# One layer-stack kernel with retrieved experts: a gather carries 32 tokens by four picks instead of 64 tokens by two

## The reference

```
q  = tb @ w_q                        # 8 heads, two halves of 128 each
s1, s2 = q @ keys1, q @ keys2        # 128 keys a half
v1, i1 = top_k(s1, 16); v2, i2 = top_k(s2, 16)
top_s, top_j = top_k(v1 + v2, 16)    # 16 of the 256 pairs, per head
gate = softmax(top_s)
act  = gelu(u_tab[expert] . t) * gate
out  = sum over 8 heads x 16 experts of act * v_tab[expert]
```

## Time and profile before

| what | value |
|---|---|
| median of 3 runs | 3376.12 us (3372.03 to 3384.19) |
| the profiled execution, its own time | 3373.29 us |
| its span | 3371.3 us |
| mean granted TensorE clock | 0.84 of 2.4 GHz |
| PE, DVE, ACT, POOL busy | 2717.7, 2109.5, 1234.6, 1221.1 us |
| moved by DMA | 1225.87 MB, mean 364 GB/s |
| products of `diag` and `ring` | 4096 instructions, 1345.2 us |

### The profile page before, as it was taken

One profiled execution on the slowest core, in us unless ns is written; L12 is line 12 of the kernel. 1 busy time (PEld: TensorE's weight loads), 2 busy tenths in 40 slices (PEclk: granted clock), 3 DMA queues, 4 the chain that ended last, 5 costly groups with the idle time before them and its releaser, 6 DMA issues.

```text
span 3371.3 us, 34626 instructions
## 1 busy us (share of the span) xinstructions
PE 2717.7 (81%) x11134; PEld 1372.6 (41%) x11134; DVE 2109.5 (63%) x4889; ACT 1234.6 (37%) x3752; POOL 1221.1 (36%) x1102
## 2 busy tenths in 40 slices
PE   8789996888988689788977789788788666666777
PEld 7767653444544145344523244344344111111133
DVE  4444688675656786565466785576556776754554
ACT  3211365442333343443333343532333343333332
POOL 0100133553433433334244433343333443433342
PEclk9989997997899689889987799797799676767676
DMA  4205698999999999999999999999999999999998
GB/s 158 75 7 192 232 402 328 392 389 377 411 406 398 391 418 383 383 377 383 413 421 421 393 413 400 376 388 422 378 412 384 390 419 421 376 422 422 421 417 333
DMA packets 186153, 1225.87 MB, mean 364 GB/s; under 512 B 21298, under 2 KB 24130, under 8 KB 50803
## 3 DMA queue, kind: packets, MB, share of 16 engines
q0 software_dynamic: 153024, 1115.00, 81.5%
q1 hardware_dynamic: 32946, 108.66, 8.5%
HBM read 1211.73 MB, written 11.84 MB: 363 GB/s over the span
## 4 chain that ended last, share of the span: by engine, by line
PE 47%; DMA 27%; DVE 15%; ACT 5%; issue 3%; DVEq 2%; POOL 1%; SPq 0%; POOLq 0%; ACTq 0%
PE ps L616 47%; DMA ring<-in_uv,picked 21%; DVE ring L2362 6%; DMA ring<-in_uv,tail_pick 4%; DVEq L2152 1%; ACT scratch L1209 1%; POOL ring L599 1%; ACT gated L1209 1%; ACT diag L1209 1%; DVE scratch L2103 1%; ACT L1209 1%; DMA scratch<-in_keys 1%; ACT act_v L1209 1%; DMA wring<-in_weights 0%; DVE scratch L2107 0%
## 5 line engine op out<-in xcount | busy, mean ns | idle before, releaser
L599 POOL DMA_INDIRECT ring<-in_uv,picked x1024 | 1143.5, 1117 | 1808.3 <-PE ps L616 1712.5
L616 PE MATMUL ps<-ring,diag 128*64 128x512 f32 x4096 | 1345.2, 751 | 490.1 <-ACT diag L1209 486.6
L2362 DVE SCALAR_TENSOR_TENSOR ring<-ring,htok 128x1024 f32<-128x1024 f32 x1024 | 1246.6, 1227 | 702.2 <-DMA ring<-in_uv,picked 697.6
L616 PE MATMUL ps<-hT,wring 128*128 128x256 f32 (+1 forms) x3200 | 797.0, 399 | 18.4 <-DVE hT L1603 8.8
L1209 ACT ACTIVATE act_v<-pre 128x1 f32<-128x1 f32 x1040 | 209.9, 202 | 1555.5 <-DVE ring L2362 1554.5
L616 PEld LDWEIGHTS ps<-ring,diag 128*64 128x64 f32 x4096 | 244.1, 156 | 1197.0 <-ACT diag L1209 1016.0
L616 PEld LDWEIGHTS ps<-hT,wring 128*128 128x128 f32 x3200 | 598.8, 194 | 323.2 <-issue 225.5
L1209 ACT ACTIVATE diag<-folded,gated 128x64 f32<-128x64 f32 x1024 | 356.1, 348 | 33.8 <-PE ps L616 0.4
L1209 ACT ACTIVATE gated<-act_v,gates 128x1 f32<-128x1 f32 x1024 | 301.6, 295 | 33.3
L616 PEld LDWEIGHTS ps<-scratch 128*128 128x128 f32 (+2 forms) x1428 | 207.1, 214 | 152.6 <-issue 89.6
L616 PE MATMUL ps<-scratch 128*128 128x128 f32 (+5 forms) x1428 | 244.2, 317 | 30.0 <-DVE scratch L1750 15.6
(11 more groups left out here) (342 smaller groups left out, 1716.5 us busy)
## 6 DMA issues: line engine op xcount, KB each, us to landing
wring<-in_weights SPq DMA_DIRECT2D x200, 512.0 KB, 7.8
ring<-in_uv,picked POOLq DMA_INDIRECT x1024, 11.8
scratch<-in_keys POOLq DMA_DIRECT2D x4, 1024.0 KB, 10.8
scratch<-in_s_gla POOLq DMA_DIRECT2D x4, 1024.0 KB, 12.3
out_o_gla<-scratch POOLq DMA_DIRECT2D x4, 1024.0 KB, 10.4
scratch<-in_s_dn POOLq DMA_DIRECT2D x1, 2048.0 KB, 12.8
scratch<-in_s_ssm POOLq DMA_DIRECT2D x1, 2048.0 KB, 17.1
out_o_dn<-scratch POOLq DMA_DIRECT2D x1, 2048.0 KB, 11.8
```

The lines of the kernel that those rows point to most:

```text
L599: pool.indirect_dma_start(out=ring[:, g % RING, :], out_offset=None, in_=io["uv"][L], in_offset=bass.IndirectOffsetOnAxis(ap=index, axis=0 ...
L616: return pe.matmul(out, lhsT, rhs, start=start, stop=stop)
L2362: stt(x, x, 1.0, h, MUL, MUL, accum_out=pre[:, g % SMALL:g % SMALL + 1]).then_inc(sem("dotted"), 1)
```

## The change

A gather now carries **32 tokens by four picks** (`FOLD` = 4, `PART` = 32). There are 32 sub-tiles of 32 gathers. `folded` is four identity matrices of 32, `diag` is 128 x 32, and `tile_v` makes four products of 256 columns (`COLS`), into partitions 0 to 31, 32 to 63, 64 to 95 and 96 to 127 of the bank. The token rows must lie four times, so `fold_rows` makes four products per half. A tile's rows are kept as two halves of 64 tokens, a half with its two column parts above each other, in three turning places (`half_rows`, one of them in `otok`). The addition to `xT` moves from slot +4 to +6 and the first fold from +6 to +8. The copies of a choice become 16 for `picked` and 16 for `gates`, of a quarter of the size, over steps 138 to 145. The final norm covers 480 tokens, its second part runs in the last sub-tile, and 32 tokens are left for `last_tile`. `iota` is now a part of `pack`, loaded and not computed. The ring keeps its seven slots.

```diff
-STEPS = 139
+STEPS = 146
+FOLD = 4
+PART = P // FOLD
+NROUND = NPICK // FOLD
+HEAD_ROUNDS = 2 * TOPK // FOLD
+COLS = 1024 // FOLD
+SUBS = FOLD * len(UNITS)
-COPY_AT, TURN_AT, FOLD_AT = 2, 4, 6
+COPY_AT, TURN_AT, ADD_AT, FOLD_AT = 2, 4, 6, 8
...
+        half_rows = (htok[:, 0, 0:512], htok[:, 0, 512:1024], otok[:, 512:1024])
+        diag = sb("diag", [P, DIAGS, PART])
+        folded = sb("folded", [P, PART])
...
-        FINAL = ((0, 256, 12, 784), (256, 192, 15, SUB_FIRST[15] + TURN_AT + 2))
+        FINAL = ((0, 256, 24, 784), (256, 224, 31, SUB_FIRST[31] + ADD_AT + 2))
...
+            def rows_of(bank, at):
+                for c in range(KD):
+                    last = mm(ps[HALF * (c // 4):HALF * (c // 4) + HALF, bank, (c % 4) * P:(c % 4 + 1) * P],
+                              hT[:, c, at:at + HALF], ident)
+                return last
+
             def first_rows():
                 pe.wait_ge(sem("score_ready"), score_no(0))
                 for b in range(2):
                     for c in range(KD):
-                        for s in range(2):
-                            last = mm(ps[HALF * s:HALF * s + HALF, 4 + 2 * b + c // 4, (c % 4) * P:(c % 4 + 1) * P],
-                                      hT[:, c, HALF * b:HALF * b + HALF], ident)
+                        for r in range(FOLD):
+                            last = mm(ps[PART * r:PART * r + PART, 4 + 2 * b + c // 4, (c % 4) * P:(c % 4 + 1) * P],
+                                      hT[:, c, PART * b:PART * b + PART], ident)
                     last.then_inc(sem("fold_mm"), 1)
-                for c in range(KD):
-                    last = pe.transpose(ps[:, c // 4, (c % 4) * P:(c % 4 + 1) * P], hT[:, c, P:2 * P], ident)
+                pe.wait_ge(sem("fold_ready"), 1)
+                for bank, at in ((0, HALF), (1, P), (4, P + HALF)):
+                    last = rows_of(bank, at)
                 last.then_inc(sem("htok_mm"), 1)
...
             def turn(w):
                 pe.wait_ge(sem("otok_ready"), w + 1)
-                for c in range(4):
+                for c in range(2):
...
-            def fold_rows(w, rows):
-                for s in range(2):
-                    last = mm(ps[HALF * s:HALF * s + HALF, w % 2, :], ident[:, HALF * (w % 2):HALF * (w % 2) + HALF], rows)
+            def fold_rows(w, h):
+                pick = ident[:, HALF * h + PART * (w % 2):HALF * h + PART * (w % 2) + PART]
+                for r in range(FOLD):
+                    last = mm(ps[PART * r:PART * r + PART, w % 2, :], pick, half_rows[w // 2 % 3])
                 last.then_inc(sem("fold_mm"), 1)
...
             def tile_v(g, w, k):
                 d, at = TILE_G.index(g) % DIAGS, D
-                for h in range(2):
-                    last = mm(ps[HALF * h:HALF * h + HALF, w % 2, :], diag[:, d, :],
-                              ring[:, g % RING, at + 512 * h:at + 512 * h + 512], k % HALF == 0, k % HALF == HALF - 1)
+                for h in range(FOLD):
+                    last = mm(ps[PART * h:PART * h + PART, w % 2, 0:COLS], diag[:, d, :],
+                              ring[:, g % RING, at + COLS * h:at + COLS * h + COLS], k % NROUND == 0, k % NROUND == NROUND - 1)
                 last.then_inc(sem("v_done"), 1)
...
-                    act.wait_ge(sem("added"), (4, 8)[p])
+                    act.wait_ge(sem("added"), (8, 16)[p])
...
-            def fold_choice(to, what, slot, g0, g1):
-                v = ids[:, what, :].rearrange("p (g s j) -> p g s j", s=2, j=TOPK)
-                for b in range(2):
-                    for r in range(2):
-                        cp(to[HALF * r:HALF * r + HALF, slot, b, g0 * TOPK:g1 * TOPK].rearrange("p (g j) -> p g j", j=TOPK),
-                           v[HALF * b:HALF * b + HALF, g0:g1, r, :])
+            def fold_choice(to, what, slot, g0, g1, subs=range(FOLD)):
+                v = ids[:, what, :].rearrange("p (g s j) -> p g s j", s=FOLD, j=HEAD_ROUNDS)
+                for b in subs:
+                    for r in range(FOLD):
+                        cp(to[PART * r:PART * r + PART, slot, b, g0 * HEAD_ROUNDS:g1 * HEAD_ROUNDS]
+                           .rearrange("p (g j) -> p g j", j=HEAD_ROUNDS), v[PART * b:PART * b + PART, g0:g1, r, :])
...
-                    if g == SUB_FIRST[w] + TURN_AT and w:
+                    if g == SUB_FIRST[w] + ADD_AT and w:
                         add_out(w - 1)
```

More of the change, by code:

```diff
@@ L145, in fold_slot @@
     at = SUB_FIRST[w - 1] + FOLD_AT
-    if w > 2 and w % 2 == 0:
-        v = [v for v in range(len(CHOICES)) if ROW_TILE[v] == w // 2 and CHOICES[v][1] != S][0]
+    if w > 2 and w % FOLD == 0:
+        v = [v for v in range(len(CHOICES)) if ROW_TILE[v] == w // FOLD and CHOICES[v][1] != S][0]
         at = max(at, topk_slot(v, rows_off(v)) + 3)
@@ L1132, in choice @@
                         pe.wait_ge(sem("score_ready"), score_no(u))
[L1133 to L1134 removed]
+                        for h in range(2):
+                            last = rows_of(4 + h, at + HALF * h)
                         last.then_inc(sem("htok_mm"), 1)
@@ L1201, in _ @@
             pe.wait_ge(sem("rows_squared"), 1)
-            for s in range(2):
-                last = mm(ps[HALF * s:HALF * s + HALF, 4, 0:1], folded[:, :], row_sum[:, 0:1])
+            for h in range(FOLD):
+                last = mm(ps[PART * h:PART * h + PART, 4, 0:1], folded[:, :], row_sum[:, 0:1])
             last.then_inc(sem("last_rows_mm"), 1)
@@ L1278, in query_copies @@
                     f(htok[:, 2, :].rearrange("p (b i) -> p b i", b=2), ps[:, 6:8, :], ACT.Copy).then_inc(sem("fold_ready"), 1)
-                    f(htok[:, 0, :].rearrange("p (b i) -> p b i", b=2), ps[:, 0:2, :], ACT.Copy).then_inc(sem("htok_ready"), 1)
+                    for half, bank in ((1, 0), (2, 1), (3, 4)):
+                        last = f(half_rows[half % 3], ps[:, bank, :], ACT.Copy)
+                    last.then_inc(sem("htok_ready"), 1)
                     for group in range(PH // GROUP - 1):
@@ L1482, in choice @@
                         act.wait_ge(sem("htok_mm"), ROW_TILE[u])
-                        act.wait_ge(sem("fold_mm"), 4 * ROW_TILE[u] - 2)
-                        last = f(htok[:, 0, :].rearrange("p (b i) -> p b i", b=2), ps[:, 4:6, :], ACT.Copy)
+                        act.wait_ge(sem("fold_mm"), 2 * (FOLD * ROW_TILE[u] - 3))
+                        for h in range(2):
+                            last = f(half_rows[(2 * ROW_TILE[u] + h) % 3], ps[:, 4 + h, :], ACT.Copy)
                         if t == 2:
```

103 lines of the change are left out of this document (48 added, 55 removed).

## The result

The changed kernel takes **3390.03 us** (median of 20 runs, 3377.32 to 3395.99), the kernel before 3376.03 us (20 runs, 3372.03 to 3386.15). The ratio is 1.0039, 95% interval 1.0029 to 1.0048: slower by 0.4%, where 3340 us was forecast.

What follows compares the result with a forecast made beforehand. Slow stretches, mostly held by TensorE returning slots late, lose 154 us of DMA transfer. Product -65, start +5, copies +14, folds +6, clock +8, tail -3.5 sum to -35.5 from 3373.3, so 3340 us beside the median; range 3302 to 3380.

Steps and rivals of the forecast that it cites:

- the product's term of -65: Slow stretches of the gather stream: shorter weighting products on TensorE win back lost transfer time, -65 us together.
- the clock's of +8: Four coupled stretches: TensorE's clock falls by some 0.05, slowing its other work, +8 us; bounds 0 and +84.
- The 45 us of the coupled stretches: 600 to 860, 1270 to 1310, 1390 to 1540, 2140 to 2260: two thirds of 68 us lost come back, 45.
- Pick at 0.64 us alone, 0.50 in a row: Weighting product: four quarters side by side take 0.65 us alone, 0.5 in a row, saving 0.43 at full clock.
- first rival: Weighting product: only two quarters run at a time, a pick still takes 0.93 to 1.1 us; 3404 us, chance 0.11.
- Copies +14, bounds 0 and 31: DVE's copies of picks and gates, 32 instead of 8 a tile: 2 us per tile, +14 us.
- Folds +6: TensorE's row folds: half folds grow from 28 to 60, with ACT's copies, +6 us.
- Start +5: Before the first pick: more identity products and transposes at 58 ns each on TensorE's chain, +5 us.
- Tail -3.5: End of the kernel: shorter last product, halved DVE passes and less store in front, -3.5 us.
- The second rival: Coupled stretches: clock stays at 0.5, +84 in place of +8, offset by -40 from picks; 3376 us, chance 0.04.
- The third: DVE takes TensorE's place: copies cost all 31 us, coupled stretches gain only a third of 68; 3376 us, chance 0.15.
- The fourth: The rest of the stream fills too, 65 + 25 us gained, no clock loss: -62, 3314 us, chance 0.15.

Runs made afterwards that it cites:

- experiment 1: The kernel before with weighting products over 256 instead of 512 columns (half of every token's sum left out), nothing else changed: 3368.61 us, ratio 0.9979.
- experiment 5: The kernel before with 256-column products (half of every sum left out) plus zero-weight 256-column products in the third and fifth scans: 3355.63 us, ratio 0.9946.

## Why the prediction was wrong

**What failed is the product's term of -65 together with the clock's of +8.** Together they were -57; experiment 1, which is just these two, measured -8. Against the terms, the product with the clock held brought -21 in place of -65, and the lost clock of two scans cost 13 to 17 in place of 8. So most of the miss is the gain, of which the runs show the size and only in part the reason; the clock is shown. Two steps made it.

- *The clock.* The step let the clock of the scans fall by 0.05, "by the rows, where clock follows busy share", and priced the rest of TensorE's work at +8. Those rows do not carry such a rule: 780 to 860 has TensorE busy 0.95 of the time at 0.76, 1270 to 1310 0.85 at 0.96. The sum is off besides: the coupled stretches have TensorE busy 471 us, not 438, so 251 us of other work, which would have made +9 and a bound of +97. The clock fell by 0.14 and 0.16 in the third and fifth scan, and TensorE's other work there grew by 22 and 25 us. The clock of 0.82 in the earlier trace rows for 1390 to 1540 was taken as that of a stretch which would hardly change; but it went with 75 us of weighting products in the scan, and the change takes a third of these away. When they were shortened the clock fell, and the untouched products became longer by about what had been saved, because their bursts went from a clock of 1.00 to 0.50 (shown for the third scan). The bound of +84 had been written down, and the value was taken near the other end. In these two scans alone the lost clock costs 13 us (experiment 5 against 1) to 17 us (with filler against without it on the changed kernel), net of the filler.
- *The gain.* The 45 us of the coupled stretches were a share of lost transfer time. With the clock held (experiment 5) the whole gain was 21 us, and in these scans nothing: TensorE spends the same time on filler. For 990 to 1060 and 2520 to 2590, where TensorE was busy throughout, 14 us were forecast. With the product alone gathers 720 to 760, which hold the second, are 5.1 us shorter; gathers 200 to 240, which hold the first, are 1.2 us longer (3.0 in experiment 5), though the whole change makes them 5.9 shorter. That part of the change's gain is thus not the product's, and where it comes from is open. The largest gain with the product alone lies at gathers 240 to 320, 7.0 us, and there the copies take it. Gathers 60 to 130 are 7.1 us longer with the product alone and 1 to 9 longer in the kernels with the change. Why that stretch gets longer with a shorter product is open, and so is why the rest of the forecast gain did not come.

The other terms:

- *Pick at 0.64 us alone, 0.50 in a row*: right, 0.64 and 0.52. So the first rival (only two quarters at a time) is out. What the step took for the halves stands in the trace of the kernel before, at a granted clock of 1.00 (two picks in a row with their weight loads, then one pick alone):

```profile
3334.75 1.94 PE L616 MATMUL ps<-ring,diag 128*64 128x512 f32 x8
3335.23 0.14 PEld L616 LDWEIGHTS ps<-ring,diag 128*64 128x64 f32 x2 [0.29 <-issue]
3335.66 0.14 PEld L616 LDWEIGHTS ps<-ring,diag 128*64 128x64 f32 x2 [0.29 <-issue]
3337.21 1.08 PE L616 MATMUL ps<-ring,diag 128*64 128x512 f32 x4 [0.53 <-ACT diag L1209]
```

  The second pick adds 0.86 us to the 1.08 of one alone, and the weights are loaded by two every 0.43 us: that is 0.43 us for two instructions of 512 columns, and about 0.2 over. A product on the whole array takes 0.24 us for 264 columns (30.46 us for 128), which by the columns would be 0.46 for 512, so the halves do stream side by side. For the quarters, which the prediction could only estimate from this, two picks take 1.04 us and one 0.64, so the second adds 0.40, where two rounds of 0.21 were taken. Their loads don't hold them up: eight issue in 0.20 us (3000.60) while the first quarter products stream, though all of them use all 128 rows.
- *Copies +14, bounds 0 and 31*: 21 measured by taking them away, 20 by doubling. The mechanism was right, and the size half as much again, inside its bounds. Its place was another than forecast: the rate at 520 to 600 fell only from 321 to 311 GB/s, and gathers 240 to 320 (1101 to 1343 us before) paid most. The duration per copy, 0.18 us, was right.
- *Folds +6*: 1 us or less by doubling them (0.8 us for 67.5 us more of TensorE's work).
- *Start +5*: the number came out (393.61 against 387.79 us for the first reissued slot), but by luck. The identity products and transposes took 7.31 us for 176, 42 ns each and not 58, so they cost 2.5 us more than before (4.8) and not 5.4 more; from their start to the first pick's product it is 42.1 us against 39.5. The other 4.6 us were there before them (they start at 350.62 against 346.02), and also in experiment 1, which leaves the start as it was:

```profile
350.60 3.71 PE L616 MATMUL ps<-masks,hT 128*64 128x128 f32 x64 [0.47 <-ACT scratch L1209]
```

  So they are not the change's. The 60 gathers that follow take 5.9 us less, and 6.6 less in experiment 1.
- *Tail -3.5*: from the issue of the last gather to the end, 29.4 us before and 24.5 after, -4.9. The parts that the prediction names add to 3.1.
- *The steady stretch*: clock near 0.5 and TensorE at 0.4 were forecast; measured 0.56 and 0.54. It costs nothing as forecast.

The second rival, the clock, had a chance of 0.04 and names the mechanism that was at work in the scans. It took the loss as offset by 40 us more of gain, which is why even it stopped at 3376. The third put the copies at all 31 us; two thirds of them were paid. The fourth's terms add to -68.5 and not to -62. Summed anew from the runs: product and clock -8, copies +21, the rest 0, +13 in all; measured +14.

## What to carry to other kernels

Before you shorten TensorE's work in a stretch where engines take turns, list what else TensorE does there and price it at the lower clock. Do not count on the stretches where it is busy throughout either: at gathers 200 to 240 the kernel with the shorter product alone took 1.2 us more. A row of an operation that the change doesn't touch (277 ns to 402 ns) is the quickest sign of it, and a busy time that stays equal though instructions got shorter is the second. And a copy on 32 rows costs nearly what one on 128 rows costs (180 and 197 ns), so finer folding multiplies every small copy by its number.

## What was not expected of the hardware

- Zero-weight products made a kernel faster: 1240 instructions of 256 columns in two scans took 17 us off (ratio 1.0039 to 0.9986), and as many of 128 columns took nothing off (1.0045).
- The same filler raised a clock of 0.85 to 0.94 in the kernel before and cost it 12 us. A higher mean clock is thus no aim in itself.
- The mean clock of a scan hides where it is low. It fell from 0.85 to 0.71, but the 128x32 products of the third scan went from 277 to 402 ns, by a factor of 1.45: their own bursts went from 1.00 to 0.50, though TensorE was busy throughout in them.
